# A two-layer hybrid attention network on one core: where the softmax sums are inverted, how many weight chunks are kept, and when tile statistics are taken

## The reference

```python
for l in range(2):
    xn = rms_norm(h, norm1_g)
    fq, fk, fv, ff, cq, ckv, krope, sq, sk, sv, gates = split(xn @ w_in)
    # fox: 8 heads of 64, every query sees all earlier keys, scores minus a running decay
    log_decay = cumsum(log_sigmoid(ff + forget_b))
    out_a = attention(rms_norm(fq), rms_norm(fk), fv, log_decay)
    # mla: 8 heads of 96, from latents cq and ckv, with rope on 32 of the 96
    out_b = attention(q_of(cq), k_of(ckv, krope), v_of(ckv))
    # swa: 8 heads of 64, meta keys and a window of 128, with a sink in the softmax
    out_c = window_attention(rms_norm(sq), rms_norm(sk), sv, sinks)
    merged = sum_over_branches(sigmoid(gates) * (out_branch @ w_branch))
    h = h + merged @ w_o
    u = conv3(rms_norm(h, norm2_g) @ w_up)
    h = h + (silu(u_gate) * u_val) @ w_down
# each attention: p = softmax(scores); out = p @ v, that is exp(s - max) @ v / sum(exp(s - max))
```

## Time and profile before

| | us |
|---|---|
| median of 3 runs | 2039.12 |
| lowest, highest | 2038.45, 2040.01 |
| the profiled execution | 2040.49 |
| its span (first to last instruction) | 2038.7 |
| PE busy in the span | 1967.0 |
| DVE, ACT, POOL busy | 1151.0, 769.5, 1019.3 |

### The profile page before, as it was taken

The page is one execution under the profiler, slowest core; times in us unless marked ns, Lnnn a source line. Parts: engine busy times, 40 slices in busy tenths (PEclk is TensorE's granted clock), DMA queues, the critical chain, the costliest instruction groups (busy, mean ns, idle before and its releaser), DMA issues.

```text
span 2038.7 us, 36672 instructions
## 1 busy us (share of the span) xinstructions
PE 1967.0 (96%) x14524; PEld 1846.7 (91%) x14524; DVE 1151.0 (56%) x2114; ACT 769.5 (38%) x1483; POOL 1019.3 (50%) x1302
## 2 busy tenths in 40 slices
PE   7899999999999999999998999999999999999999
PEld 7788898888999999999997888988889999999987
DVE  7665466677465656652256654666774656656411
ACT  5455565555233222220134555655552332222100
POOL 6754544443444544454466555444434445454553
PEclk9999999999999999999999999999999999999999
DMA  4212111111232332233232111111112323333332
GB/s 154 63 43 63 53 53 53 53 42 53 63 126 73 94 94 94 83 94 97 91 116 63 44 62 53 53 53 53 43 52 65 124 83 96 92 94 94 104 94 93
DMA packets 44799, 156.28 MB, mean 77 GB/s; under 512 B 5010, under 2 KB 5266, under 8 KB 44628
## 3 DMA queue, kind: packets, MB, share of 16 engines
q1 hardware_dynamic: 44484, 153.71, 24.0%
q10 hardware_dynamic: 144, 0.22, 0.0%
HBM read 149.58 MB, written 4.26 MB: 75 GB/s over the span
## 4 chain that ended last, share of the span: by engine, by line
PE 78%; DVE 11%; ACT 5%; issue 3%; POOL 2%; DMA 0%; DVEq 0%; ACTq 0%; POOLq 0%
PE ps L1304 20%; PE ps L1307 19%; PE ps L1309 19%; PE ps L1537 5%; PE ps L1323 3%; PE ps L1319 2%; PE ps L1315 2%; PE ps L1318 2%; DVE osum L1935 2%; PE ps L1444 1%; DVE rstd L1641 1%; PE ps L1483 1%; DVE ps L1905 1%; POOL wl L792 1%; PE ps L1489 1%
## 5 line engine op out<-in xcount | busy, mean ns | idle before, releaser
L792 POOL TENSOR_TENSOR wl<-raw,wh 128x256 fp32r<-128x256 f32 x1076 | 797.5, 773 | 713.9 <-DVE wh L1620 704.7
L1304 PE MATMUL ps<-xh,wh 128*128 128x264 f32 (+1 forms) x2880 | 811.6, 303 | 14.3 <-DVE wl L1699 10.4
L1307 PE MATMUL ps<-xl,wh 128*128 128x264 f32 (+1 forms) x2880 | 764.9, 285 | 0.0
L1309 PE MATMUL ps<-xh,wl 128*128 128x264 f32 (+1 forms) x2880 | 585.3, 285 | 0.0
L1304 PEld LDWEIGHTS ps<-xh,wh 128*128 128x128 f32 x2880 | 547.5, 190 | 38.1 <-issue 26.3
L1307 PEld LDWEIGHTS ps<-xl,wh 128*128 128x128 f32 x2880 | 547.6, 190 | 15.2 <-issue 6.7
L1309 PEld LDWEIGHTS ps<-xh,wl 128*128 128x128 f32 x2880 | 451.8, 190 | 0.0
L1620 DVE CAST wh<-raw 128x1024 fp32r<-128x1024 f32 x270 | 201.0, 745 | 183.1 <-PE ps L1304 103.1
L1927 DVE TENSOR_TENSOR ps<-ps,cst 128x128 f32<-128x128 f32 (+6 forms) x240 | 70.8, 296 | 189.1 <-PE ps L1489 135.8
L1537 PE MATMUL ps<-pt,vx 128*128 128x256 f32 (+5 forms) x448 | 145.3, 404 | 0.8 <-ACT pt L1221 0.7
L1221 ACT ACTIVATE pt<-ps 128x256 f32<-128x256 f32 (+5 forms) x224 | 78.1, 363 | 113.3 <-DVE ps L1927 112.1
(11 more groups left out here) (192 smaller groups left out, 3445.6 us busy)
## 6 DMA issues: line engine op xcount, KB each, us to landing
raw<-weights SPq DMA_DIRECT2D x270, 512.0 KB, 3.5
h<-tokens SPq DMA_DIRECT2D x4, 528.0 KB, 6.9
h<-tokens SPq DMA_DIRECT2D x8, 264.0 KB, 4.9
residual<-h SPq DMA_DIRECT2D x8, 264.0 KB, 4.8
h<-residual SPq DMA_DIRECT2D x8, 264.0 KB, 5.0
out<-h SPq DMA_DIRECT2D x8, 256.0 KB, 4.4
cst<-constants SPq DMA_DIRECT2D x1, 1008.0 KB
extra<-positions SPq DMA_DIRECT2D x17, 4.1 KB
```

The costliest lines, as they stand in the source:

```text
L792: ins = nc.gpsimd.tensor_tensor(wl[c % SPLIT][:, part], raw[:, c % RAW, part], wh[c % SPLIT][:, part].bitcast(F32), ALU.subtract)
L1304: a = nc.tensor.matmul(out, a_hi, x_hi[:, sl], start=first, stop=False)
L1307: nc.tensor.matmul(out, a_hi, x_lo[:, sl], start=False, stop=False)
L1309: ins = nc.tensor.matmul(out, a_lo, x_hi[:, sl], start=False, stop=last)
```

## The change

1. **Inverse of the softmax sums.** The four reciprocals are gone. ACT gets a step `inverse` one block ahead of where the first reciprocal stood: logarithm of `osum` into a new tile `inverse`, then exponential with scale −1, which is a guess of 1/osum. DVE does a Newton step on it three and four blocks behind, in two operations over 528 columns: osum·inverse, then (that − 2)·inverse, which is minus the refined inverse. The heads multiply becomes an operation with scalar −1 that turns the sign back, and stands two blocks later (`LAG`).
2. **One ring of chunks.** `RAW` goes from 2 to 4, and `wl` gets no buffers of its own: POOL writes the low part over `raw` in place. A buffer is free when PE has done with it, so the load of chunk n (n ≥ 4) waits until PE has started chunk n−3 (`s_start`, shown as chunk_started) in place of the split of chunk n−2. In SP's program the load that stands at the first block of chunk c is that of chunk c+3, where it was c+4.
3. **Statistics by kind of tile.** A table `LATE` delays the statistic, the Newton step and the norm of sk by one block and of cq by two, and the transposes of fv by one.
4. **Tables.** `BEGIN`, `ORDER`, `START`, `FIRST_LEAD` and `LAG` have other numbers: among them gF0 stands ahead of fv0, decay2 has offset 15 + 1 in place of 16 + 2, extras 7 in place of 11, rope 19 + 2 (25 − 1), and job 0's maxima begin 16 blocks ahead of it in place of 18.

```diff
-RAW, SPLIT = 2, 3
+RAW, SPLIT = 4, 3
-FIRST_LEAD, FIRST_STEP = 18, 1.0
-START = [13, 16, 11, 25, 25, 29, 12]
+FIRST_LEAD, FIRST_STEP = 16, 1.0
+START = [12, 15, 7, 18, 19, 26, 9]
+LATE = {"sk": 1, "cq": 2, "fv": 1}
-            put(e + STAT_LAG, 3, "stat", t)
-            at = e + NORM_LAG
+            late = LATE.get(t.kind, 0)
+            put(min(e + STAT_LAG + late, next_in_slot[t.i] - 1), 3, "stat", t)
+            at = e + NORM_LAG + late
...
-        for q in range(4):
-            put(i + q, 6, "recip", j, q)
+        put(i - 1, 6, "inverse", j)
+        put(i + 2, 6, "recip", j, 0)
+        put(i + 3, 6, "recip", j, 1)
...
+    wl = sb("wl", [P, RAW, CW], F32R, offset=raw_at)
-    wl = [sb(f"wl{i}", [P, CW], F32R) for i in range(SPLIT)]
...
-                    sp.wait_ge(s_lo, n - RAW + 1)
+                    sp.wait_ge(s_start, n - RAW + 2)
...
-                    load(n // BLK + AHEAD + RAW)
+                    load(n // BLK + RAW - 1)
...
+                    elif s[0] == "inverse":
+                        j = s[1]
+                        logarithms()
+                        act.wait_ge(heads_copied.sem, heads_copied.at(l, j, 1))
+                        act.wait_ge(meta_heads_copied.sem, meta_heads_copied.at(l, j))
+                        if j > 0:
+                            act.wait_ge(heads_ready.sem, heads_ready.at(l, j - 1))
+                        follows(nc.scalar.activation(inverse[:, :], osum[:, :], ACT.Ln))
+                        nc.scalar.activation(inverse[:, :], inverse[:, :], ACT.Exp, scale=-1.0).then_inc(
+                            inverse_guess.sem, inverse_guess.tick((l, j)))
...
-                        nc.vector.reciprocal(osum[:, a:a + T // 4], osum[:, a:a + T // 4]).then_inc(
-                            dve_step.sem, dve_step.tick((l, "recip", j, q)))
+                            nc.vector.tensor_tensor(osum[:, :], osum[:, :], inverse[:, :], ALU.mult).then_inc(
+                                dve_step.sem, dve_step.tick((l, "recip", j, 0)))
+                            nc.vector.scalar_tensor_tensor(out=osum[:, :], in0=osum[:, :], scalar=-2.0, in1=inverse[:, :],
+                                                           op0=ALU.add, op1=ALU.mult).then_inc(
+                                dve_step.sem, dve_step.tick((l, "recip", j, 1)))
...
-                        nc.vector.tensor_tensor(oraw[:, :], oraw[:, :], osum[:, :], ALU.mult).then_inc(
+                        nc.vector.scalar_tensor_tensor(out=oraw[:, :], in0=oraw[:, :], scalar=-1.0, in1=osum[:, :],
+                                                       op0=ALU.mult, op1=ALU.mult).then_inc(
```

More of the change, by code:

```diff
@@ L86 @@
 ZEROS = 10
-FIRST_LEAD, FIRST_STEP = 18, 1.0
-START = [13, 16, 11, 25, 25, 29, 12]
-LAG = {("dve", "layer stat"): 1, ("dve", "M"): 1, ("dve", "MM"): 1, ("act", "O"): -1, ("pool", "high"): -1, ("act", "head copy"): 1, ("dve", "STM"): -1, ("dve", "decay2"): 2, ("pool", "extras2"): -1, ("dve", "rope"): -1, ("dve", "square low"): 1, ("act", "inverse"): 2}
+FIRST_LEAD, FIRST_STEP = 16, 1.0
+START = [12, 15, 7, 18, 19, 26, 9]
+LAG = {("dve", "layer stat"): 1, ("dve", "M"): 1, ("dve", "MM"): 1, ("act", "O"): -1, ("pool", "high"): 1, ("act", "head copy"): 1, ("dve", "decay2"): 1, ("act", "tanh"): -1, ("dve", "rope2"): 1, ("dve", "decay"): 1, ("dve", "turn"): 1, ("dve", "rope"): 2, ("dve", "heads"): 2, ("act", "VT"): -1}
+LATE = {"sk": 1, "cq": 2, "fv": 1}
 def constants():
@@ L256, in mixer_plan @@
         if t.kind in ("fv", "sv", "mv"):
-            put(e + 3, 3, *place(("VT", t, 0)))
-            put(e + 4, 3, *place(("VE", t, 0)))
+            late = LATE.get(t.kind, 0)
+            put(e + 3 + late, 3, *place(("VT", t, 0)))
+            put(e + 4 + late, 3, *place(("VE", t, 0)))
         if t.kind == "sv":
@@ L388, in build @@
     xl = sb("xl", [P, KD, T], F32R)
+    raw_at = at[0]
     raw = sb("raw", [P, RAW, CW])
+    wl = sb("wl", [P, RAW, CW], F32R, offset=raw_at)
     wh = [sb(f"wh{i}", [P, CW], F32R) for i in range(SPLIT)]
-    wl = [sb(f"wl{i}", [P, CW], F32R) for i in range(SPLIT)]
     h_at = at[0]
@@ L443, in build @@
     hsum = sb("hsum", [P, T])
+    inverse = sb("inverse", [P, T])
     cg = sb("cg", [P, 2, T], offset=late_at)
@@ L561, in build @@
     heads_ready = S("heads_ready")
+    inverse_guess = S("inverse_guess")
     heads_high = S("heads_high_part")
@@ L726, in _ @@
             sp.dma_start(extra[0:2, :], POS[0, :, :]).then_inc(s_cst, 16)
-            for n in range(2, AHEAD + RAW):
+            for n in range(2, RAW - 1):
                 load(n)
@@ L791, in chunk_low @@
                     part = slice(a, a + CW // 4)
-                    ins = nc.gpsimd.tensor_tensor(wl[c % SPLIT][:, part], raw[:, c % RAW, part],
+                    ins = nc.gpsimd.tensor_tensor(wl[:, c % RAW, part], raw[:, c % RAW, part],
                                                   wh[c % SPLIT][:, part].bitcast(F32), ALU.subtract)
@@ L1296, in weights @@
                 a = n % BLK * P
-                return wh[c % SPLIT][:, a:a + P], wl[c % SPLIT][:, a:a + P]
+                return wh[c % SPLIT][:, a:a + P], wl[:, c % RAW, a:a + P]
             def gemm(n, slot, x_hi, x_lo, first, last, skip=0):
@@ L1698, in _ @@
                     dve.wait_ge(s_hi, 1)
-                    nc.vector.tensor_tensor(wl[0][:, :], raw[:, 0, :], wh[0][:, :].bitcast(F32), ALU.subtract).then_inc(
+                    nc.vector.tensor_tensor(wl[:, 0, :], raw[:, 0, :], wh[0][:, :].bitcast(F32), ALU.subtract).then_inc(
                         s_lo, 1)
```

16 lines of the change are left out of this document (8 added, 8 removed).

## The result

| | before | changed |
|---|---|---|
| median of 9 runs, us | 2039.12 | 2043.72 |
| lowest to highest | 2036.23 to 2041.79 | 2038.25 to 2045.48 |
| profiled execution, its span | 2040.49, 2038.7 | 2044.70, 2042.9 |
| PE busy in the span | 1967.0 | 1966.4 |

The changed kernel takes 1.0023 times as long, with a 95% interval of 1.0015 to 1.0031. The forecast was 2032.6, 6.5 us faster; it is 4.6 us slower. The time is inside the range that was given, and the sign is wrong.

A forecast was written before the change was run, and what follows sets the result against it. PE, busy for 96% of the span, was taken as the bound. Terms −10.0 − 3.4 + 6.9 + 2 − 2 = −6.5 on 2040.5, less 1.4, gave 2032.6 us; own range 2026 to 2037, reaching 2016 and 2049.

The forecast's parts named there:

- The inverse, −10.0: Mixers, eight windows behind DVE reciprocals: 10 of PE's 12.8 us idle won; bounds 5 and 12.8.
- the 3 that I named as the sign: Eight windows behind reciprocals: PE's idle time was to fall from 12.8 to about 3 us.
- Price on DVE: DVE, per job: two new operations cost 1.6 to 3.0 us against 3.8 for reciprocals, saving 0.8 to 2.2.
- ACT, +2: ACT, 1.3 us more per job: +2 us for all 24 jobs; bounds 0 and +8.
- my sign's 2 us: PE waits that end on ACT were to stay within 2 us of before.
- The tables, −2: Delays and order of last gates and mla tiles: −2 us, bounds −8 and +6; no row told which waits go.
- The layer's start, +6.9: Both layers' starts: chunk 6 load behind the decay wait stalls PE at the value tile; +6.9 us, bounds −8 and +12.
- The clock, −3.4: Half-clock stretches of 6.8 us behind 317 and at 1335: one of two goes, −3.4 us; bounds 0 and −6.8.
- My own sign: Mixers: prediction wrong without the `vt` stall, or if PE's idle time does not fall outside it.
- The ring elsewhere, 0: Chunk loads away from the layer's start: no cost, with a cover of 2.4 us.
- Rival C: Ahead of guesses and high parts, ACT late by 1.3 us per job: +8 in place of +2, 2038.6 us; chance 0.14.
- rival A: Layer's start: chunk 6 load +11, reciprocals −5, no clock stretch won, ACT +2; slower, 2047 us; chance 0.23.

The follow-up runs named there:

- e1: Kernel before with the ring of chunks alone, tables and reciprocals as before: 2037.41 us, ratio 1.0001.
- e2: Kernel before with the ring and the inverse, old tables kept: 2041.42 us, ratio 1.0015.
- e6: Changed kernel with four reciprocals back on DVE and no inverse on ACT, all else as changed: 2038.01 us, ratio 0.9995.
- e10: e9 with the order from tile gS2 on and the last two jobs' begins (391, 436) as in the kernel before: 2024.41 us, ratio 0.9927.
- e12: e10 without the ring: two buffers of raw, three of the low part, loads that wait for the split: 2024.78 us, ratio 0.9937.
- e11: Changed kernel, extras at offset 11, order from gS2 and last two begins as before, last tangents behind the inverse: 2031.92 us, ratio 0.9962.
- e9: Changed kernel with reciprocals back on DVE and extras at offset 11: 2035.56 us, ratio 0.9982.
- e3: Changed kernel with extras at offset 11 again in place of 7: 2035.02 us, ratio 0.9987.
- e5: e2 with the tangent of the last four gates' first pair four blocks later on ACT, behind the inverse: 2034.51 us, ratio 0.9975.

## Why the prediction was wrong, point by point

- **The inverse, −10.0: wrong, and the step that failed.** I took PE's idle time behind reciprocals as their price, 10 of 12.8 us. e1 against e2 shows that only 5.2 us of it go when the reciprocals do. In the changed kernel it is less still: the same eight places, shifted with their jobs, have 9.3 us left instead of the 3 that I named as the sign, and with the reciprocals put back under the same tables (e6) they have 10.6. So the new tables alone close about 2 of the 12.8, and the inverse closes 1.3. What I had left out is what the inverse opens elsewhere, which is more: in sum it costs the changed kernel 5.7 us (e6) where I had 10 won, and this difference alone is larger than the 11 by which the forecast missed. My lower bound of 5 was not worked out from its reason (1.0 us at each of eight places allows up to 8) and did not hold. The places in the changed kernel, then in e6:

```profile
sum 80.30, PE 70.97 PEld 64.33 DVE 63.72 ACT 51.73 POOL 45.88; mean PE 8.87 PEld 8.04 DVE 7.96 ACT 6.47 POOL 5.73
```

```profile
sum 80.30, PE 69.70 PEld 62.80 DVE 64.97 ACT 47.24 POOL 40.91; mean PE 8.71 PEld 7.85 DVE 8.12 ACT 5.91 POOL 5.11
```

- The gain of 5.3 and 6.7 us between blocks 144 and 320 does not need the inverse. e6 and e10, which have reciprocals, gain 5.0 and 6.6 there against the kernel before, and so does e12 (5.1 and 6.7) without the ring. It is the tables: the wait of 0.9 us for `ptm` at 242, with two that follow it closely, is gone, and the one of 0.9 at 187 is 0.3 in e10. That the fourth job begins five blocks later is the likely reason, and no run has that number alone.
- **Price on DVE: right.** The operations' means in the changed kernel (busy us, mean ns | idle before):

```profile
L1959 DVE SCALAR_TENSOR_TENSOR osum<-osum,inverse 128x528 f32<-128x528 f32 x24 | 27.9, 1161 | 0.2
L1955 DVE TENSOR_TENSOR osum<-osum,inverse 128x528 f32<-128x528 f32 x24 | 22.1, 922 | 13.6 <-ACT inverse L1169 13.5
...
L1169 ACT ACTIVATE inverse<-inverse 128x528 f32<-128x528 f32 x24 | 15.5, 646 | 0.8
```

  0.92 + 1.16 = 2.1 us per job against 3.8, inside the forecast's 1.6 to 3.0. The surcharge beside POOL is there (a mean of 1.16 for the second operation and 0.92 for the first, 0.71 where POOL is idle, as in e2 at 575.83, and up to 1.7 and 1.8 where it works), while the reciprocals of the kernel before stay between 0.91 and 0.98. It is in line with the Trainium skill ("SBUF — State Buffer", section "Who interferes with whom"), whose rule spoke against this change; here it took 0.7 us of a job's saving, not the whole.
- **ACT, +2: mis-sized, and in the wrong place.** 1.3 us per job was right (2 x 0.65 above). PE's waits that end on ACT even stayed in my sign's 2 us (18.6 before, 19.5 in the changed kernel), because the tables took some of them away while the inverse opened others. But I spread it evenly. It falls on two tiles per layer (`sq`), on the second job's transposes (in e11 2.6 us against 2.0 in e10), and above all on the last job, where the tangents force two table loads ahead of it: 3.9 us per layer in e2. The changed kernel begins its last job nine blocks earlier and has no such wait, but pays 2.7 and 2.8 us for the early maxima.
- **The tables, −2: wrong sign at the end, too small in the middle.** −12.0 in the middle; +10.9 for blocks 320 to 448. Moving that part back (e9 to e10) gave 11.1. The two nearly cancel, so the net of this term is near my −2 by luck. With the inverse the same move, with four tangents shifted, brings this stretch back by 8.8, but the whole time only by 3.1 (e3 to e11). I had no row for it and said so, and my bound of +6 would not have held for the last two jobs. The order could have told me: in DVE's program the last job's maxima now stand directly behind the last normed tile's Newton step. I had looked only at the waits for `rawt` there, and these stayed (9.0 to 9.3).
- **The layer's start, +6.9: mechanism right, size close.** Stall, place and order of events are as forecast: DVE's wait was 4.57 (about 4 named), PE's for `vt` 3.8 and 5.4 (8 named, but 2.1 and 1.7 of it show as a wait for the gate just ahead). It came to +5.1. The chain was shorter than summed: decay2 took 4.9 us and not 5.8, landing 3.5 and not 4, rope 2.5 and not 3.5. Against what the new tables could have had, the price of the load's place is 4.9 and 5.2 us of idle time (the table at e9), and 8.7 or 2.5 of the whole time (e3, e9).
- **The clock, −3.4: wrong.** Both stretches of 6.8 us at 0.50, near 317 and 1337, are still there.
- **My own sign.** I wrote that the prediction is wrong if PE's idle time in the mixers does not fall outside the stall at `vt`. It was 67.0 us, 59.3 without the old waits for POOL, and is 71.8, 58.8 without `vt` and `merged`: it fell by 0.5 where I had 10.
- **The ring elsewhere, 0: right** (e1, e12).
- Rival C, ACT late ahead of a tile's work, names part of what happened, though its 2038.6 is 5.1 us low; rival A had the direction (2047; its sum leaves out the −2 of the tables and would be 2045), with the load's +11 at +5.1. None had the last job's place, the largest single loss. That the time lies inside my range says little, since the range took in A and B.

## What to carry to other kernels

An operation moved off a busy engine is worth what PE waits for *after* it is gone, which is less than the idle time behind it, and the engine that receives it has its own places where nothing may be added: find them first (here two squares per layer, and the one job that meets a change of activation tables). What such a move is worth also hangs on the tables around it: the inverse came out 3 to 5 us faster with the old tables and one tangent moved (e5), and between nothing and 7.5 slower with the new ones (e3 and e9, e6, e10 and e11). In a queue worked in order, ask of each DMA that waits which load stands behind it; one number there was worth some 5 us of PE's idle time. And when a change mixes a mechanism with re-tuned tables, undo each alone, and then two together: here the tables up to gS2 were worth 14 us, the tables behind it cost 11 with reciprocals, and single results did not add up.
